# The next head pair's projections as slices inside the RWKV-7 steps, and the sample tokens in a compact form

## What is computed

```python
def _wkv_step(S, inp):
    r, w, k, v, kk, kka = inp
    sa = jnp.einsum('bhij,bhj->bhi', S, -kk)
    S = S * w[:, :, None, :] + sa[..., None] * kka[:, :, None, :] + v[..., None] * k[:, :, None, :]
    y = jnp.einsum('bhij,bhj->bhi', S, r)
    return S, y
...
    p = p + (shifted - p) * lp['mu_shift']
    r, k, v, xw, xa, xg = jnp.split(p, RWKV_SPLITS, axis=-1)
...
    S, y = lax.scan(_wkv_step, S0.astype(f32), seq)
```

## Time and profile before

| | |
|---|---|
| median of 3 runs | 4362.78 us (4361.63 to 4368.57) |
| the profiled execution | 4369.68 us, span 4368.1 us |
| PE busy over the span | 3960.5 us (91%) |
| DVE busy | 3024.6 us (69%) |
| ACT, POOL busy | 1459.7 us (33%), 1473.3 us (34%) |
| mean granted PE clock | 0.937 of 2.4 GHz |
| from the first step of pair 0 to that of pair 7 | 498.64 to 1521.29 us |

### The profile page before, as it was taken

One profiled execution on the slowest core, in us unless ns is written; L12 is line 12 of the kernel. 1 busy time (PEld: TensorE's weight loads), 2 busy tenths in 40 slices (PEclk: granted clock), 3 DMA queues, 4 the chain that ended last, 5 costly groups with the idle time before them and its releaser, 6 DMA issues. The chain is left out here.

```text
span 4368.1 us, 72112 instructions
## 1 busy us (share of the span) xinstructions
PE 3960.5 (91%) x29289; PEld 3760.7 (86%) x29289; DVE 3024.6 (69%) x3965; ACT 1459.7 (33%) x2056; POOL 1473.3 (34%) x778
## 2 busy tenths in 40 slices
PE   4897899899989687979999999999988999999997
PEld 3896787788778577969999999999988999999996
DVE  1565454555455533348996888888768999999996
ACT  1343321222122111142223444444424444444333
POOL 0332322332332120003365444444443444444441
PEclk7998998999899678989999999999999999999998
DMA  8221222222222124222248999999989999999994
GB/s 371 83 90 52 80 77 93 82 96 77 83 91 86 47 71 171 77 81 78 93 158 319 388 372 382 384 381 368 385 342 356 377 380 387 382 380 377 365 357 176
DMA packets 214273, 982.33 MB, mean 225 GB/s; under 512 B 21952, under 2 KB 101952, under 8 KB 106560
## 3 DMA queue, kind: packets, MB, share of 16 engines
q1 hardware_dynamic: 92256, 524.19, 31.5%
q0 software_dynamic: 57984, 409.37, 23.9%
q10 hardware_dynamic: 63840, 46.15, 3.2%
HBM read 917.54 MB, written 62.09 MB: 224 GB/s over the span
## 5 line engine op out<-in xcount | busy, mean ns | idle before, releaser
L93 PE MATMUL PS<-first_HH,tail_WH 128*128 128x352 f32 (+1 forms) x3072 | 976.7, 318 | 55.8 <-DVE first_HL L1746 31.7
L95 PE MATMUL PS<-first_HH,tail_WL 128*128 128x352 f32 (+1 forms) x3072 | 960.7, 313 | 0.0
L94 PE MATMUL PS<-first_HL,tail_WH 128*128 128x352 f32 (+1 forms) x3072 | 958.6, 312 | 0.0
L93 PE MATMUL PS<-dn_BH,tail_WH 128*128 128x352 f32 x2048 | 669.6, 327 | 34.4 <-DVE dn_BL L2326 23.9
L95 PE MATMUL PS<-dn_BH,tail_WL 128*128 128x352 f32 x2048 | 661.4, 323 | 0.0
L94 PE MATMUL PS<-dn_BL,tail_WH 128*128 128x352 f32 x2048 | 659.6, 322 | 0.0
L93 PEld LDWEIGHTS PS<-first_HH,tail_WH 128*128 128x128 f32 x3072 | 584.8, 190 | 60.6 <-issue 32.0
L2302 POOL DMA_INDIRECT dn_VR<-in_v_rows,tail_EI x192 | 436.3, 2273 | 573.6 <-DVEq L2345 552.2
L2051 POOL DMA_INDIRECT up_UR<-in_u_rows,tail_EI x192 | 420.1, 2188 | 505.2 <-DVEq L2132 485.7
L94 PEld LDWEIGHTS PS<-first_HL,tail_WH 128*128 128x128 f32 x3072 | 585.2, 190 | 0.5
L95 PEld LDWEIGHTS PS<-first_HH,tail_WL 128*128 128x128 f32 x3072 | 584.6, 190 | 0.0
(11 more groups left out here) (401 smaller groups left out, 7462.0 us busy)
## 6 DMA issues: line engine op xcount, KB each, us to landing
tail_WR<-in_peer_u SPq DMA_DIRECT2D x128, 1024.0 KB, 9.1
tail_WR<-in_peer_v SPq DMA_DIRECT2D x128, 1024.0 KB, 8.3
mix_RING<-in_w_ada SPq DMA_DIRECT2D x88, 1024.0 KB, 4.9
mix_RING<-in_w_in SPq DMA_DIRECT2D x37, 1024.0 KB, 4.8
tmp_z<-up_ZB ACTq DMA_DIRECT2D x128, 176.0 KB, 8.0
tmp_gd<-up_STG ACTq DMA_DIRECT2D x22, 1024.0 KB, 18.3
dn_GG<-tmp_gd SPq DMA_DIRECT2D x16, 1408.0 KB, 10.3
dn_ZI<-tmp_z SPq DMA_DIRECT2D x128, 176.0 KB, 6.3
```

What stands on the lines that cost most here:

```text
L93: nc.tensor.matmul(out, r32(wh), r32(xh), start=first, stop=False)
L94: nc.tensor.matmul(out, r32(wh), r32(xl), start=False, stop=False)
L95: return nc.tensor.matmul(out, r32(wl), r32(xh), start=False, stop=last)
```

## The change

- `pe_fill` puts tiles 0 and 1 of pair i+1 inside the levels of steps 0 and 1 of pair i: seven slices per step (3, 3, 2, 2, 2, 2, 2 of 16 k-tiles, both halves), one between z and t of each level and one behind t.
- Tile 2 of pair i+1 and the low-rank projections go into the scan of step 1 (first half of the tokens) and behind the mean in `pe_post` (second half). Nothing is left between the head sums.
- Step 2 is gone. The 32 sample tokens are solved in a compact form (`ST` = 32): products of 64 x 64 (L1079 of the new file), a fixed-point solve of four rounds (`pe_solve`, `dve_solve`), and one product for the new states. All eight chunks of the scan of step 1 run there.
- ACT and POOL split weights in half tiles (`high`, `low` with `part`), at other places: tile 0 in the preparation, tile 1 early in step 1 ahead of POOL's first mask, tile 2 in the sample stage. POOL also takes two operations of 1024 columns.
- `prep_rows` takes the v rows last, behind a wait for tile 2 of the pair.
- SP loads the weight tiles and the modulation tiles in a new order.
- In `phase_down` the PE loop over groups is unrolled.

```diff
+            def pair(i, ahead):
 
                 for t in range(1, ADA_PAIR):
-                    sp.wait_ge(ada_used, ADA_PAIR * i + t)
...
+                    if ahead and t in (3, 6):
+                        sp.wait_ge(proj_done, 6 * i + 6 + t // 3)
+                        load_tile(i + 1, t // 3)
+                    next_ada(i, t)
...
+                pair(i, True)
+                sp.wait_ge(proj_done, 6 * i + 11)
+                load_low(i + 2)
...
+                load_ada(i + 1, 0)
+                sp.wait_ge(proj_done, 6 * i + 12)
+                load_tile(i + 2, 0)
...
+        def pe_fill(pe, i, step, slot):
+
+            at, n = ((0, 3), (3, 3), (6, 2), (8, 2), (10, 2), (12, 2), (14, 2))[slot]
+            mm = project(pe, i + 1, step, range(at, at + n), ((0, 4), (1, 5)))
+            if slot == 6:
+                mm.then_inc(proj_done, 1)
+
...
+                if ahead:
+                    if lv == 1:
+                        pe.wait_ge(x_ready, 2 * u + 2)
+                    pe_fill(pe, i, step, 2 * lv - 2)
...
+                    pe_scan(pe, i, step - 1, 2 * lv - 1)
+                if ahead and lv < last:
+                    pe_fill(pe, i, step, 2 * lv - 1)
+            pe_modulation(pe, i, 3 * step + 2)
+            if ahead:
+                pe.wait_ge(proj_ev, 6 * i + (7 + step))
 
...
+        def pe_solve(pe, i, n):
+
+            if n == 0:
+                pe.wait_ge(asr_ready, i + 1)
+                pe.wait_ge(m4_ready, i + 1)
+                pe.wait_ge(uv_ready, i + 1)
+                for h in range(2):
+                    at = slice(64 * h, 64 * h + 64)
+                    nc.tensor.matmul(PS[0:ST, 3, at], ASR[:, 0, :], IDENT[:, at], start=True, stop=False)
+                    mm = nc.tensor.matmul(PS[0:ST, 3, at], M4[ST:2 * ST, h, 0, :], UV[ST:2 * ST, at], start=False, stop=True)
+            else:
+                pe.wait_ge(u_ready, 4 * i + n)
+                for h in range(2):
+                    at = slice(64 * h, 64 * h + 64)
+                    mm = nc.tensor.matmul(PS[0:ST, 3, P + 64 * h:P + 64 * h + 64], M4[0:ST, h, 0, :],
+                                          (BB if n == 1 else UV)[0:ST, at], start=True, stop=True)
+            mm.then_inc(u_done, 1)
+
+        def pe_samples(pe, i, ahead):
+
+            pe.wait_ge(y0_ready, 4 * i + 4)
             pe.wait_ge(si_in, 32 * i + 32)
+            for b in range(NB):
+                mm = nc.tensor.matmul(PS[:, 4, 2 * NS * b:2 * NS * b + 2 * NS], SI[:, b, :],
+                                      SLT[:, KA_:KR_ + 1, NS * b:NS * b + NS], start=True, stop=True)
+            mm.then_inc(sa_done, 1)
+            pe_turn(pe, i, 1)
+            pe.wait_ge(gk_read, 2 * i + 2)
+            for h in range(2):
+                rows = slice(64 * h, 64 * h + 64)
+                mm = nc.tensor.matmul(PS[0:2 * ST, h, 0:2 * ST], SLT[rows, KB_:KK_ + 1, :].rearrange("p k t -> p (k t)"),
+                                      SLT[rows, KA_:KR_ + 1, :].rearrange("p k t -> p (k t)"), start=True, stop=True)
+            mm.then_inc(sm_prod, 1)
+            nc.tensor.matmul(PS[0:2 * ST, 2, 0:P], SLT[:, KBH:KKH + 1, :].rearrange("p k t -> p (k t)"), IDENT[:],
+                             start=True, stop=True)
+            nc.tensor.matmul(PS[ST:2 * ST, 2, P:2 * P], SLT[:, KV_, :], IDENT[:], start=True, stop=True).then_inc(st_done, 1)
+            pe.wait_ge(gk_ready, 2 * i + 2)
+            pe.wait_ge(mod_read, 3 * i + 2)
...
+                pe_scan(pe, i, 1, n)
+                if n < 4:
+                    pe_solve(pe, i, n)
+                if n in (0, 1):
+                    pe_modulation(pe, i, 6, 8 * n, 8 * n + 8)
+                if n in (4, 5):
+                    pe_modulation(pe, i, 7, 8 * n - 32, 8 * n - 24)
+                if n == 4:
+                    pe.wait_ge(u_ready, 4 * i + 4)
+                    for h in range(2):
+                        rows = slice(64 * h, 64 * h + 64)
+                        mm = nc.tensor.matmul(PS[rows, 4, 2 * ST:3 * ST], UV[:, rows], M4[:, h, 1, :], start=True, stop=True)
+                    mm.then_inc(ys_done, 1)
+                if n == 5:
+                    pe.wait_ge(um_ready, i + 1)
+                    pe.wait_ge(vm_ready, i + 1)
+                    for half in range(2):
+                        mm = nc.tensor.matmul(PS[:, 2 + half, :], BKT[:], UVM[:, 4 * half:4 * half + 4, :], start=True,
+                                              stop=True)
+                    mm.then_inc(so_prod, 1)
+                if ahead and n < 3:
+                    if n:
+                        pe.wait_ge(proj_ev, 6 * i + (8 + n))
+                    project_low(pe, i + 1, n, 0)
+                if ahead and n >= 3:
+                    project(pe, i + 1, 2, range(3 * n - 9, 3 * n - 6 if n < 7 else KT), ((0, 6),))
+            pe_turn(pe, i, 2)
+
...
+        def pe_post(pe, i, ahead):
 
             pe.wait_ge(yt_ready, 3 * i + 3)
+            if ahead:
+                pe.wait_ge(proj_ev, 6 * i + 11)
             for half in range(2):
                 mm = nc.tensor.matmul(PS[:, 0 + half, 0:TH], BDM[:], YT[:, TH * half:TH * half + TH], start=True, stop=True)
             mm.then_inc(mean_done, 1)
-            if ahead2:
-                project(pe, i + 2, 0, (1,))
+            if ahead:
+                project(pe, i + 1, 2, range(KT), ((1, 7),)).then_inc(proj_done, 1)
...
-            def pair(i, ahead, ahead2):
-                if ahead:
-                    project(pe, i + 1, 1)
+
+            def pair(i, ahead):
                 pe.wait_ge(banks_idle, i + 1)
                 head_sum(pe, sq_ready, i + 1, ss_done)
-                if ahead:
-                    project(pe, i + 1, 2)
                 head_sum(pe, rk_ready, i + 1, bo_done)
-                if ahead:
-                    project_low(pe, i + 1)
-                    pe.wait_ge(proj_ev, 6 * i + 12)
                 pe.wait_ge(prep_ready, i + 1)
-                for step in range(3):
-                    pe_step(pe, i, step)
-                pe_samples(pe, i, ahead2)
-                pe_post(pe, i, ahead2)
-
-            for i in range(NPAIR - 2):
-                pair(i, True, True)
-            pair(NPAIR - 2, True, False)
-            pair(NPAIR - 1, False, False)
-
-
-        def act_step(act, i, step, ahead2):
...
+        def act_samples(act, i, ahead):
+            A = nc.scalar.activation
+            act.wait_ge(sa_done, i + 1)
+            A(ASR[:].rearrange("p k (b s) -> p k b s", s=NS),
+              PS[:, 4, 0:2 * ST].rearrange("p (b k s) -> p k b s", k=2, s=NS), ACT.Copy).then_inc(asr_ready, 1)
+            act.wait_ge(st_done, i + 1)
+            A(BKT[:], PS[0:2 * ST, 2, 0:P], ACT.Copy)
+            A(UV[ST:2 * ST, :], PS[ST:2 * ST, 2, P:2 * P], ACT.Copy).then_inc(uv_ready, 1)
+            if ahead:
+                evacuate(act, i + 1, 3, 0, 3)
+                high(act, i + 1, 2, 0)
+                evacuate(act, i + 1, 4, 0, 4)
+                high(act, i + 1, 2, 1)
+                evacuate(act, i + 1, 5, 0, 5)
+                decay(act)
+            act_rows_of(act, i, 2)
+
+        def act_step(act, i, step, ahead):
...
+            if ahead and step == 1:
+                for part in range(2):
+                    high(act, i + 1, 1, part)
...
+            if ahead:
+                evacuate(act, i + 1, step, 4, 1 + step)
...
+                if ahead:
+                    evacuate(act, i + 1, 2, 6, 6)
...
+                    for part in range(2):
+                        low(pool, i + 1, 0, part)
+                for step in range(2):
+                    u = 2 * i + step
+                    if ahead and step == 1:
+                        for part in range(2):
+                            low(pool, i + 1, 1, part)
...
+                pool.wait_ge(si_in, 32 * i + 32)
+                G.tensor_tensor(SO[:], SI[:], bcast(PI[:, PC0 + NS:PC1:NS + 1], 2, P), ALU.mult)
+                pool.drain().then_inc(so_pre, 1)
+                pool.wait_ge(uv_ready, i + 1)
+                G.tensor_tensor(UVM[ST:2 * ST], bcast(UV[ST:2 * ST, :], 1, NB), bcast(SEL8[ST:2 * ST, :], 2, P),
+                                ALU.mult)
+                pool.drain().then_inc(vm_ready, 1)
+                if ahead:
+                    for part in range(2):
+                        low(pool, i + 1, 2, part)
...
+            def mixed(which, kt, dst):
+
                 V.tensor_tensor(DT[:, body], PP[:, which, 0:W1 - 1], PP[:, which, 1:W1], ALU.subtract)
                 dve.drain()
                 V.scalar_tensor_tensor(dst, DT[:, body], PARAM[:, bass.ds(i + (PAR["mu"] + kt), 1)], PP[:, which, 1:W1],
                                        ALU.mult, ALU.add)
                 dve.drain()
-                if which == 1:
-                    dve.sem_inc(act_rows, 1)
-            dve.sem_inc(pp_used, 1)
-
+
+            mixed(0, 0, RR[:, body])
+            mixed(1, 8, KX[:, body])
+            dve.sem_inc(act_rows, 1)
```

(33 more changed lines are left out.)

414 lines of the change are left out of this document (175 added, 239 removed).

## The result

| | before | after |
|---|---|---|
| median | 4365.24 us (4 runs, 4361.63 to 4368.57) | 4448.59 us (4 runs, 4436.30 to 4455.40) |
| ratio | | 1.0188, 95% interval 1.0161 to 1.0215 |
| the profiled execution | 4369.68 us | 4436.30 us, span 4434.7 us |
| PE busy over the span | 3960.5 us | 3910.1 us |
| first step of pair 0 to that of pair 7 | 1022.65 us | 1126.20 us |

The change makes the kernel 1.9% slower; 3.2 us less was forecast. Profile against profile it is 66.6 us more, median against median 83.4: the profiled execution of before lay above the median of its runs, that of after is the shortest of its four.

The account below looks back on a forecast made before the run. PE and DVE both fill the preparation, with DVE's chain its floor; PE is dense in the steps. Seven periods +41.5, prologue -22.3, last pair -22.4: -3.2 us, giving 4366.5 profiled, 4359.5 on the median; range 4322 to 4397.

Parts of the forecast that it names:

- Preparation: From the mean to the next pair's step 0: 36.5 us, bounds 34.3 to 41, against 40.17, so -3.7.
- the collision: In the preparation, POOL's two weight-split halves of tile 0 slow DVE products beside them: +2.0 us, between 0 and 4.6.
- Step 0 and step 1: Steady pair's two steps with slices added: 42.4 us (+11.7) and 46.4 us (+11.8), 12.4 of matmuls each less small holes.
- Rival 1: Step 0's first two slices: clock stays down, 4.6 us more a pair, 32 in all, 4391 us; chance 0.25.
- rival 3: Step 1: tile 1's weights load late, levels start late; 5 us late gives +35, 4395 us; chance 0.06.
- Samples: Compact sample stage replacing step 2: 27.0 us, bounds 23 to 33, against 41.25, so -14.3.
- one half of that, +2.5, bounds 0 to 7: Sample stage's low-clock term: half of the old stretch's 14 of 41.25 us at 1.2 GHz, taken as +2.5 us.
- rival 2: No POOL collision in the preparation (-2.0) and sample stage at full clock (-2.5): -31 in all, 4328 us; chance 0.28.
- Last pair: Final pair's sample stage: 40.98 us become 18.6, -22.4, bounds -18 and -26.
- Prologue: Ahead of step 0 of pair 0: DVE's 15.96 us wait gone and smaller savings, -22.3 us, bounds -16 and -23.
- phase_down: Unrolling its PE loop: no effect, bounded by 5 us if fetched instructions come late.
- The rule weighed in the prediction: Waits inside a loop make the next matmuls cold, losing half the throttled time; by it the sum comes 4 us higher.

Follow-up runs that it names:

- e8: Changed kernel with 24 more wide products, results unread, between the sample stage's lead and its first chunk; 4418.89 us, one run.
- e2: Kernel before with phase_down's TensorE loop written out and nothing else changed; 4377.69 us, ratio to before 1.0031.
- e10: e1 with 96 increments of an unused semaphore on TensorE ahead of phase_down's loop; 4438.28 us, ratio to before 1.0171.
- e1: Changed kernel with phase_down's TensorE loop back as a hardware loop; 4465.28 us, ratio to before 1.0241.
- e4: Kernel before with compact samples but no slices, first half of tile 0 in chunks 0 to 4 of the sample stage; 4334.62 us, ratio 0.9927.

## Why the prediction was wrong

Against the sum of -3.2 us the profile has +66.6, 69.8 us more. Over the seven periods 1126.20 - 1022.65 = 103.5 us were added in place of 41.5, which is 62 of the 69.8. Against what was forecast for each stage, those 62 are 54 in the seven sample stages, 5.5 in the preparations, 5 in step 1 and -3 in step 0. The steps in turn:

- **Preparation**, 36.5 forecast, 37.3 measured. Right, the collision too: 2.0 us (2.70 for 0.73).
- **Step 0 and step 1**, 42.4 and 46.4 forecast, 41.6 and 46.0 measured. Right; in pairs 0 to 2 step 1 took 1.4 to 3.3 us more, with 3.4 to 6.9 more of it at the lower clock in two of them. The slices cost what they are long less the holes, and covered nothing. Rival 1 did not happen in step 0: the granted clock over its first 20 us was 0.70 to 0.84, not under 0.6. Nor did rival 3: in step 1 PE waited 2.1 us once for the turn of the modulation and otherwise 1.7 us in all, none of it for weights. "DVE, ACT and POOL are a third full or less" in the steps was misread: the earlier trace rows have POOL at 13.11 of 30.72 us and DVE at 15.70 of 34.63. Nothing in the sum rests on it.
- **Samples**, 27.0 forecast, 35.5 measured. This is the step that failed, in one term: "one half of that, +2.5, bounds 0 to 7" for the low clock. The low stretch is 24.00 us (20.5 in pairs 0 to 2) and costs 10.6 by e8's chunks, past the bound of 7; less the 2.5 allowed, that is 8.1 of the 8.5 us by which the stage was longer than forecast. The other terms together were right: 24.5 without the clock, against 24.9 (35.5 less 10.6) and 25.5 in e8. The share came from the old step 2, and the prediction gives no reason why half of it should hold in a stage of other products; its arithmetic was short as well, since 14 us at the lower level cost 7 and half of that is 3.5. A sign was at hand: the last pair's step 2 has no projection products in it, and its clock was 0.72 where a steady pair had 0.83. Rival 1 named the mechanism, but at step 0; rival 2 assumed the contrary here. The mark I had set, "a sample stage of 31 or more with ACT's sigmoid as releaser", was half met: the length, not the releaser. The wait for ACT shows only at the full clock, 0.64 us in e8, inside the "+1.0, bounds 0 to 3" taken for it.
- **Last pair**, -22.4 forecast. To the next phase -14.1 was measured (130.0 before, 115.9 after), with the sample stage at 25.7 us and a granted clock of 0.61 in place of 18.6: mostly the same term again, and outside the bounds of -18 and -26.
- **Prologue**, -22.3 forecast, -24.5 measured: step 0 of pair 0 began at 474.1. About right, 1.5 us past the bound of -23.
- **phase_down**, 0 forecast, bound 5; measured +10.0, with phase_up at -9.4 in the same execution. Most of it is the loop: written out, phase_down took 8.4 us more in e2 than before (1029.8, 1021.4) and 6.6 more than in e10 (1031.4, 1024.8). But the question was put wrongly. What the loop costs depends on its place, which every edit ahead of it moves: left as a loop, the changed kernel would have been at e1's 4465.

The rule weighed in the prediction (the Trainium skill, TensorE: Matmul & The Clock Gate, HAM oscillation) speaks of waits in a loop. In the sample stage the trace does not agree with waits as the reason: PE had one wait of 0.39 us ahead of the fall and none in the 24 us at 1.2 GHz, and in e8, behind the same wait (0.40), it stayed at 2.4 GHz in three pairs. That a low stretch costs half its length is nearly so: 0.44 here.

As for the purpose: two tiles' blocks and the low-rank products beside the preparation cost 5.1 us there. Moved out, they freed 2.9 us (40.17 to 37.3) and cost 22.3 in the two steps (10.9 and 11.4). The compact samples were worth 16 us a pair by themselves, with the wide products early: step 2 took 41.25 us and e4's stage 24.7 in five pairs of six. The changed kernel spent that.

## What to carry to other kernels

Leave filler work beside an engine that is the floor of its stretch; where the receiving stretch is dense on the same engine, the work costs its whole length. When a stage is made shorter by making its matmuls smaller, price it at the lower clock first, and put the wide products early in it; then look at the clock of the stages behind it too. Before judging a change that alters the amount of code, compare the other phases and the packets of the instruction queue: 65 us of gain or loss came from nothing but the place of a loop.
